# Key tiles of the shared keys and values made once, root rows instead of root columns in the sparse query stage, and identity products in the openings of a two-block transformer kernel

## The reference, cut to what matters

```python
def shared_kv(h, ...):                     # once, between the two layers
    u = modulate(rms_norm(h, kv_norm_g), shift, scale)
    kv = (u @ w_kv).reshape(b, s, 3, 2, N_KV_HEADS, HEAD_DIM)
    k_cmp = rms_norm(compress(kv[:, :, 0, 0], 0), kv_k_gain[0])   # silu(blocks @ phi_w1) @ phi_w2
    v_cmp = compress(kv[:, :, 0, 1], 1)
    k_slc = rope(rms_norm(kv[:, :, 1, 0], kv_k_gain[1]));  v_slc = kv[:, :, 1, 1]
    k_win = rope(rms_norm(kv[:, :, 2, 0], kv_k_gain[2]));  v_win = kv[:, :, 2, 1]
...
def nsa_mixer(u, ...):                     # the sparse attention
    qg = u @ w_qg
    q = rms_norm(qg[..., :hdim].reshape(b, s, N_HEADS, HEAD_DIM), q_gain)
    gates = jax.nn.sigmoid(qg[..., hdim:])
```

## Time and profile before

| what | value |
|---|---|
| median of 3 runs | 3850.7 us |
| profiled execution | 3850.64 us, of it span from the first to the last instruction 3848.9 us |
| mean granted TensorE clock | 0.971 of 2.4 GHz |
| PE busy | 3637.3 us (95%) |
| DVE busy, ACT busy | 1914.3 us (50%), 1422.3 us (37%) |
| DMA | 360.8 MB, 94 GB/s |

### The profile page before, as it was taken

The page is one execution under the profiler, slowest core; times in us unless marked ns, Lnnn a source line. Parts: engine busy times, 40 slices in busy tenths (PEclk is TensorE's granted clock), DMA queues, the critical chain, the costliest instruction groups (busy, mean ns, idle before and its releaser), DMA issues.

```text
span 3848.9 us, 49990 instructions
## 1 busy us (share of the span) xinstructions
PE 3637.3 (95%) x19328; PEld 2934.7 (76%) x19328; DVE 1914.3 (50%) x3874; ACT 1422.3 (37%) x2510; POOL 107.7 (3%) x183
## 2 busy tenths in 40 slices
PE   7879999989998999999999989999899998889999
PEld 6669956778887888777777768888788886668887
DVE  5757735555456545555545444333433345764332
ACT  3251212432233222555555543223322233863222
POOL 0000000010001000000000000000000000000000
PEclk9879999989998999999999999999899999999999
DMA  6200026234543544111111112222222221012222
GB/s 240 93 1 1 1 87 228 102 117 178 181 169 123 190 175 155 69 66 51 50 50 51 70 56 93 91 99 99 90 82 93 93 74 45 2 43 75 90 100 77
DMA packets 47159, 360.82 MB, mean 94 GB/s; under 512 B 5216, under 2 KB 5600, under 8 KB 28128
## 3 DMA queue, kind: packets, MB, share of 16 engines
q1 hardware_dynamic: 23472, 270.36, 19.1%
q0 software_dynamic: 23472, 87.50, 6.8%
HBM read 355.74 MB, written 2.10 MB: 93 GB/s over the span
## 4 chain that ended last, share of the span: by engine, by line
PE 84%; DVE 8%; issue 3%; ACT 3%; DVEq 1%; DMA 0%; PEld 0%; ACTq 0%; PEldq 0%; POOL 0%; SPq 0%; POOLq 0%
PE bank L798 21%; PE bank L803 21%; PE bank L804 21%; PE bank L1618 4%; PE bank L760 2%; PE bank L1951 1%; PE bank L1968 1%; PE bank L1939 1%; PE bank L2419 1%; PE bank L2386 1%; PE bank L1927 1%; DVE w_lo_sb L1220 1%; PE bank L778 1%; PE bank L2408 1%; PE bank L727 1%
## 5 line engine op out<-in xcount | busy, mean ns | idle before, releaser
L798 PE MATMUL bank<-x_hi_sb,w_hi_sb 128*128 128x512 f32 x2888 | 1155.2, 400 | 58.6 <-DVE w_lo_sb L1220 15.2
L804 PE MATMUL bank<-x_hi_sb,w_lo_sb 128*128 128x512 f32 x2888 | 1133.2, 392 | 0.0
L803 PE MATMUL bank<-x_lo_sb,w_hi_sb 128*128 128x512 f32 x2888 | 1132.8, 392 | 0.0
L798 PEld LDWEIGHTS bank<-x_hi_sb,w_hi_sb 128*128 128x128 f32 x2888 | 546.8, 189 | 208.8 <-issue 72.3
L1043 ACT ACTIVATE w_hi_sb<-slab_sb 128x1024 fp32r<-128x1024 f32 (+2 forms) x549 | 500.9, 936 | 502.7 <-PE bank L798 315.6
L1220 DVE TENSOR_TENSOR w_lo_sb<-slab_sb,w_hi_sb 128x1024 fp32r<-128x1024 f32 (+2 forms) x549 | 573.5, 1076 | 182.0 <-ACT w_hi_sb L1043 167.1
L804 PEld LDWEIGHTS bank<-x_hi_sb,w_lo_sb 128*128 128x128 f32 x2888 | 546.3, 189 | 117.4
L803 PEld LDWEIGHTS bank<-x_lo_sb,w_hi_sb 128*128 128x128 f32 x2888 | 547.5, 190 | 108.1
L1386 DVE TENSOR_TENSOR hid_sb<-silu_gate_sb,bank 128x512 f32<-128x512 f32 x110 | 75.6, 688 | 605.2 <-PE bank L804 605.2
L798 PE MATMUL bank<-hid_hi_sb,w_hi_sb 128*128 128x512 f32 x880 | 343.0, 390 | 0.0
L804 PE MATMUL bank<-hid_hi_sb,w_lo_sb 128*128 128x512 f32 x880 | 342.8, 390 | 0.0
(11 more groups left out here) (349 smaller groups left out, 3786.6 us busy)
## 6 DMA issues: line engine op xcount, KB each, us to landing
slab_sb<-weights SPq DMA_DIRECT2D x80, 2048.0 KB, 7.8
keep_sb<-ada POOLq DMA_DIRECT2D x133, 512.0 KB, 4.5
slab_sb<-weights SPq DMA_DIRECT2D x44, 1536.0 KB, 6.4
slab_sb<-weights SPq DMA_DIRECT2D x20, 1280.0 KB, 6.1
tables_sb<-ada POOLq DMA_DIRECT2D x14, 512.0 KB, 6.2
work_sb<-ada POOLq DMA_DIRECT2D x13, 512.0 KB, 7.6
h_sb<-x SPq DMA_DIRECT2D x4, 512.0 KB, 7.4
out<-h_sb SPq DMA_DIRECT2D x8, 256.0 KB, 2.7
```

The source lines that it names most:

```text
L798: mm = pe.matmul(out, w_hi[p][:, w], hi, start=first, stop=False)
L803: pe.matmul(out, w_hi[p][:, w], lo, start=False, stop=False)
L804: return pe.matmul(out, w_lo[p][:, w], hi, start=False, stop=last)
```

## The change

The weights of the two key projections are no longer written twice: one slab holds the selected key tile, the window key tile and the two compression tiles, and the values have a slab of their own (`w_v`). The second copies of the key heads are made by ACT at the end of the query stage. In the query stage the roots of a half are split into a high and a low part, turned into 16 rows (4 transposes), copied to SBUF by ACT, and each tile's bank is filled by one float32r product with a selector `pick`. The values take their banks one at a time. The two extra sums before the second opening are spread over the last products, one of them behind the stage's end. Identity products are added at twelve places. Cut to its core:

```diff
-    ("w_kv", 2, 4096),
+    ("w_kv", 1, 4096),
+    ("w_v", 1, 2048),
...
+        pick = sb("pick", [P, 4 * P], F32R)
+        root_parts = sb("root_parts", [P, NB, 16], F32R)
...
-        def pe_cols(e, sqv, tiles, nb, by_tile, sub):
+        def pe_cols(e, sqv, tiles, nb, by_tile, sub, busy):
...
             mm.then_inc(e.A.full[s], 1)
+            pe_stay_busy(e, busy)
             pe.wait_ge(inverted, e.nth(inverted))
...
+        def pe_turn_roots(e, ring, seat):
+            pe = e.eng
+            pe.wait_ge(parts_ready, e.nth(parts_ready))
+            s = e.give(ring, seat)
+            for b in range(NB):
+                mm = pe.transpose(ring.bank[s][0:16, b * P:(b + 1) * P], root_parts[:, b, :].bitcast(F32), ident)
+            mm.then_inc(ring.full[s], 1)
+        def pe_spread_rows(e, ring, seat, rows, j):
+            if j == 0:
+                e.eng.wait_ge(roots_turned, e.nth(roots_turned))
+            s = e.give(ring, seat)
+            n = S // len(rows)
+            for i, r in enumerate(rows):
+                mm = e.eng.matmul(ring.bank[s][:, i * n:(i + 1) * n], pick[0:16, j * P:(j + 1) * P], r, start=True, stop=True)
+            mm.then_inc(ring.full[s], 1)
+        def act_root_rows(e, ring, seat, rows):
...
+                x = act.activation(r, ring.bank[s][0:16, i * n:(i + 1) * n], ACT.Copy)
+            x.then_inc(roots_turned, 1)
+            act.drain().then_inc(ring.free[s], 1)
+        def dve_root_parts(e, src, tiles, sub):
...
+            e.link(dve.tensor_copy(hi, src), dve_step)
+            dve.tensor_tensor(lo, src, hi.bitcast(F32), ALU.subtract).then_inc(parts_ready, 1)
...
-            seats = [e.give(e.A, e.acc)] * NB if together else [e.give(e.A, e.acc) for _ in range(NB)]
+            seats = [e.give(e.A, e.acc)] * NB if together else []
             for i in range(parts):
                 p = e.take(part, e.part)
                 for b in range(NB):
+                    if len(seats) == b:
+                        seats.append(e.give(e.A, e.acc))
...
                     if sums and half == 1 and n == KT // 2 - 1:
+                        late = [lambda: pe_sums_open(e, cross, True),
+                                lambda: cross is not None and pe_sums_of(e, 1, cross[0])]
...
-            pe_cols(e, sq, 8, NB, False, 1)
+            pe_stay_busy(e, 16)
+            pe_cols(e, sq, 8, NB, False, 1, 18)
...
-            pe_cols(e, sq, 4, NB, False, 1)
+            pe_stay_busy(e, 10)
+            pe_cols(e, sq, 4, NB, False, 1, 6)
...
             e.stage_end("w_in")
+            pe_stay_busy(e, 40)
             e.stage_end("rope_tables")
             pe_swap(e, b1_qk, 6, wait=False)
+            pe_stay_busy(e, 20)
...
             e.stage_end("w_co")
+            pe_stay_busy(e, 4)
             pe_sums_close(e, crosses[0])
+            pe_stay_busy(e, 5)
             pe_rms_spread(e, rms=rms_add)
             pe_rms_spread(e)
+            pe_stay_busy(e, 20)
             pe_ffn(e, cross=crosses[1])
             e.stage_end("ffn_down")
-            pe_sums_close(e, crosses[1])
+            pe_stay_busy(e, 4)
+            pe_sums_close(e, crosses[1], (2,))
+            pe_stay_busy(e, 5)
             pe_rms_spread(e, rms=rms_add)
             pe_rms_spread(e)
+            pe_stay_busy(e, 20)
...
             pe_parts_opening(e, x_hi, x_lo)
             e.slab.next()
-            for _ in range(2):
-                pe_tile_parts(e)
-            pe_settle(e)
-            pe_head_cols(e, kv_sq, 4)
             pe_token_parts(e, 2, 2 * P, 2 * P)
             pe_settle(e)
-            pe.wait_ge(inverted, e.nth(inverted))
-            for j in range(4):
-                pe_spread(e, NB, 2, j)
+            pe_head_cols(e, kv_sq, 2)
...
             pe_slab(e, (), 0, 0, None, more=[compress])
-            pe_swap(e, kv_raw, 4)
+            pe.wait_ge(inverted, e.nth(inverted))
+            for j in range(2):
+                pe_spread(e, NB, 2, j)
+            pe_swap(e, kv_raw, 2)
...
             pe_head_cols(e, q_sq[:, 0:4, :], 4)
             pe_tile_parts(e)
             pe_settle(e)
-            pe.wait_ge(inverted, e.nth(inverted))
+            pe_turn_roots(e, e.A, e.acc)
+            pe_tile_parts(e)
             for j in range(4):
-                pe_spread(e, NB, 2, j)
-            pe_tile_parts(e)
+                pe_spread_rows(e, e.A, e.acc, rows_sparse, j)
...
-            pe.wait_ge(inverted, e.nth(inverted))
+            pe_turn_roots(e, e.A, e.acc)
             for j in range(4):
-                pe_spread(e, NB, 2, j)
+                pe_spread_rows(e, e.A, e.acc, rows_sparse, j)
```

More of the change, by code:

```diff
@@ L375, in two_blocks @@
         ident, ones1 = K("ident"), K("ones")[:, 0:1]
+        rows_dilated = [w_hi[i][0:16, QKV_PART:D] for i in (2, 3)]
+        rows_sparse = [root_rows[0:16, :]]
         acc = Ring(sem, "acc", 4)
@@ L819, in pe_parts @@
                         pe.wait_ge(ready, e.nth(ready))
-                    if late is not None and (t, kt) == (tiles - 1, nkt - 2):
-                        late()
+                    if late is not None and t == tiles - 1 and kt >= nkt - len(late):
+                        late[kt - nkt]()
                     mm = pe_product(e, s, p, slice(at * P, (at + 1) * P), hi[:, kt, :], lo[:, kt, :],
@@ L935, in pe_stay_busy, with pe_sums_of, pe_sums_open @@
                 e.eng.matmul(turn_bank[1][:, 0:P], ident, ident, start=True, stop=True)
-        def pe_sums_open(e, cross=None):
+        def pe_sums_of(e, n, tile):
+            for b in range(NB):
+                at = n * NB + b
+                e.eng.matmul(e.S.bank[e.sums][:, at:at + 1], tile[:, b * P:(b + 1) * P], ones1, start=at == 0, stop=False)
+        def pe_sums_open(e, cross=None, first=False):
             pe = e.eng
@@ L942, in pe_sums_open, with pe_sums_close @@
                 pe.wait_ge(summed, e.nth(summed))
-            for n, tile in enumerate([sq_sum] if cross is None else [sq_sum, cross[0], cross[1]]):
-                for b in range(NB):
-                    at = n * NB + b
-                    pe.matmul(e.S.bank[e.sums][:, at:at + 1], tile[:, b * P:(b + 1) * P], ones1, start=at == 0, stop=False)
-        def pe_sums_close(e, cross=None):
+            pe_sums_of(e, 0, sq_sum)
+            if cross is not None and not first:
+                pe_sums_of(e, 1, cross[0])
+                pe_sums_of(e, 2, cross[1])
+        def pe_sums_close(e, cross=None, left=()):
             pe = e.eng
+            for n in left:
+                pe_sums_of(e, n, cross[n - 1])
             for _ in range(KT):
@@ L1150, in act_ffn, with dve_invert @@
                 e.acc.pos += KT
-        def dve_invert(e, cols, factor=1.0, some=None):
+        def dve_invert(e, cols, factor=1.0, some=None, parts=None):
             dve = e.eng
@@ L1160, in dve_invert @@
                 r = dve.tensor_scalar(inv[:, 0:some], inv[:, 0:some], factor, None, ALU.mult)
-            r.then_inc(inverted, 1)
+            if parts is None:
+                r.then_inc(inverted, 1)
+            else:
+                e.link(r, dve_step)
+                parts(inv[:, 0:cols])
         def dve_add_normed(e, src, gain, after=None):
@@ L3095, in dve_run @@
             order = Order(e, KV_USES)
-            for q in range(PARTS):
-                dve_w_lo(e, q, D)
+            for q in range(2):
+                dve_w_lo(e, q, D, 1)
+            order.go("c1")
+            s = e.take(e.A, e.acc)
+            for kv in range(2):
+                for odd in range(2):
+                    dve.tensor_copy(kv_cmp[64 * odd:64 * odd + 64, 1, kv, 0:S - odd],
+                                    bank[s][64 * kv:64 * kv + 64, odd:S])
+            dve.drain().then_inc(e.A.free[s], 1)
             dve.wait_ge(hidden_ready, 1)
```

73 lines of the change are left out of this document (48 added, 25 removed).

## The result

The changed kernel takes 3824.63 us, the median of 4 runs (3823.66 to 3825.36), against 3850.41 us for the kernel before (4 runs, 3845.92 to 3850.93): a ratio of 0.9935 with a 95% interval of 0.9918 to 0.9953. The forecast was 3820 us with a range of 3808 to 3833. The profiled execution took 3824.53 us, 26.1 us under that of before, where the sum of the terms had said 30.3.

What follows compares the result with a forecast made beforehand. The prediction took PE, busy 95% of the span, and its time at the low granted clock to bound the kernel. Its terms summed to -30.3 us, from 3850.64 to 3820.3, rounded to 3820 us, range 3808 to 3833.

Steps and rivals of the forecast that it cites:

- (d): Rival, delta net: weight loads don't follow the clock, so gains of 3.8 and 3.0 us go; 3827 us, chance 0.04.
- (e): Rival, sparse queries: the row spreads' detour through DVE, PE and ACT eats what they save; 3822 us, chance 0.04.
- (a): Rival, keys' stage: gains only its two tiles, -10.9 us, as something else holds the next SwiGLU; 3828 us, chance 0.12.
- shared keys and values: Main term, keys' stage: two tiles, half the head sums, two spreads and low-clock time leave PE's path; -19.0 us.
- sparse queries: Query stage: first half's 64 spread passes become 4 transposes and 4 float32r products, second half +0.2 us; -1.7 us.
- delta net, first stage: Delta net preparation: identity products start the single-column burst high and let the spreads run high; -5.8 us.
- delta net, end: Delta net's end: 10 products make 32 passes run mostly high, six more overrun a short wait; -2.2 us.
- opening after w_co: First opening: added products on the path and overrunning a wait, against a faster opening behind; +0.5 us.
- opening after the first SwiGLU: Second opening: eight passes moved, added products' cost against spreads and opening partly at the high clock; -0.5 us.
- (c): Rival, identity products: they lift no clock and overrun short waits by 8.9 us; 3838 us, chance 0.08.
- (b): Rival, clock: the bursts hold the high level throughout, and so do the openings behind; 3799 us, chance 0.10.
- (f): Rival, slower: identity products run at the low level everywhere and overrun their waits, +28.7 us; 3858 us, chance 0.02.

Runs made afterwards that it cites:

- e1: The changed kernel without any of the identity products the change added; 3829.04 us, ratio 0.9946.
- e3: The changed kernel with the sparse queries' inverse roots spread by columns again, 64 passes a half; 3825.39 us, ratio 0.9936.
- e2: The changed kernel with the keys' 16 two-column head sums ahead of the values' 96 products instead of behind them; 3818.02 us, ratio 0.9917.
- e6: e2 with single identity products between every eight single-column products of the delta net's bursts, 3 in the first, 1 in the second; 3821.55 us, ratio 0.9929.
- e4: The kernel before with only the keys made once and the values' banks one by one; no row spreads, no added identity products; 3834.28 us, ratio 0.9957.
- e8: e2 with the second compression's weights in the values' slab, so the next SwiGLU's first weights load and split earlier; 3810.97 us, ratio 0.9902.
- e11: e9 without the 18 identity products behind the delta net's first burst, the 16 ahead kept; 3809.41 us, ratio 0.989.
- e7: e2 without the delta net's added identity products (16 and 18 in preparation, 10 and 6 at its end); 3824.37 us, ratio 0.9936.
- e5: e2 without the identity products added to the two openings (4, 5 and 20, twice); 3813.36 us, ratio 0.9905.
- e9: e8 without the identity products added to the two openings; 3808.82 us, ratio 0.9894.
- e12: e9 with two identity products between every four single-column products of the delta net's bursts, 14 in the first, 6 in the second; 3814.26 us, ratio 0.9907.
- e10: e9 without the rotary stage's 40 and 20 identity products; 3807.67 us, ratio 0.9896.

## Why the prediction was right, and where it was not

The total is inside the range, 4.6 us from the forecast. Three rivals are nearer by their number, (d) 3827, (e) 3822 and (a) 3828 us, but none describes what the traces show. That the sum came so near is in part luck: the terms that name an edit gained 22.9 of the 30.3 us, and stretches that no edit touches gave another 3.2. By its own steps, against the profiled execution:

| step | forecast | measured | by |
|---|---|---|---|
| shared keys and values | -19.0 | -13.2 | stretch; the same in e1 and e3 |
| sparse queries | -1.7 | -1.2 | stretch; -1.2 in e1, -1.1 in e2 |
| values' banks | -0.9 | -1.1 | stretch; in all 13 kernels |
| rotary stage | -0.9 | -1.4 | -0.9 to -1.5 in the others with it, 0.0 without |
| delta net, first stage | -5.8 | -4.6 | -6.2 to -6.5 in six others |
| delta net, end | -2.2 | -2.8 | to the middle of w_out; -0.6 to -2.8, -3.6 in e6 |
| opening after w_co | +0.5 | +0.6 | mean of six +1.1 |
| opening after the first SwiGLU | -0.5 | +1.0 | mean of six +0.3 |
| start | +0.2 | -0.3 | with the first stage |
| stretches that the change doesn't touch | 0 | -3.2 | see below |

**The step that failed** is the main term, -19.0 forecast and -13.2 measured. The parts that leave PE's path were costed rightly (18.0 forecast, 18.6 measured at the compression's start), and so was DVE's 1.2 us. The value products ran high, too. What failed is that the working ends there, with the 3.4 us at 0.50 gone, and puts what the moved burst does to the work behind it at nothing. The burst of head sums didn't vanish: now the compression stood directly behind it, and its price stayed at the 7.36 us of the earlier trace rows, which it had with 96 value products and 64 spreads ahead. It took 12.17 us, the spreads behind it 1.5 us more. Putting the sums back ahead of the values (e2) gave 19.9 us: the forecast's term was the price of an order that the change didn't write. e4 shows that it has nothing to do with the identity products.

**Rival (a)** gave a nearer size for this stretch (-10.9) for the wrong reason. More than the two tiles came through (half the head sums and all four early spreads did), and the compression and the spreads then gave 6.3 us back. Its mechanism, another hand-over that sets the end, is real all the same, and comes next: with the slab freed early the DMA is off the path, and ACT's and DVE's order holds the SwiGLU. e8 took that for another 4.9 us.

**The delta net** went by the mechanism named: the burst starts high and falls on the way, the spreads run high. Two sizes were off. The forecast let each microsecond at the high level save one; by its own prices (0.116 and 0.215 us) it saves 0.85, so its 3.8 us were worth 3.2, and the burst gained 2.7. And of the 3.0 us for the spreads half can come without the 18 products (8.82 us in e11) or without any (8.85 in e4), depending on when the level rises. The 18 products overran the reciprocal (done at 254.24, spreads from 255.48) by 1.2 us, close to the 1.0 forecast. Of the gain, 1.2 to 1.7 us are given back in the core behind, in every kernel but e1 and e7; e4, which came to it only 2.5 us earlier, gave back 1.3. Why is not shown.

**The openings** were forecast at 0 together. The measured cost of their products is 2.3 us, and leaving them out was right (e5, e9). In the timeline of the first opening the loss is the 4 products at the low level (1.92 us) and the 5 that overrun a short wait (2.48 against 0.57), more than the faster spreads (2.63 against 3.78) and the faster start of the SwiGLU give back.

**Rival (d),** weight loads that don't follow the clock, is refuted more sharply than by the rows of before. In e12 eight single-column passes took 0.95 us at 1.00 and 1.71 us at 0.50, in one burst: 0.119 against 0.214 us a pass.

```profile
242.60 0.95 PE L720 MATMUL bank<-const_sb,sq_sb 128*128 128x1 f32 x8
...
244.29 1.71 PE L720 MATMUL bank<-const_sb,sq_sb 128*128 128x1 f32 x8
```

The Trainium skill, TensorE: Matmul & The Clock Gate, section LDWEIGHTS (loading the stationary operand), gives columns over 1.2 GHz for a load, 107 ns for these 128 columns, with no clock level in it; the trace is near that at the high level and has twice that at the low one.

Of the others, (c) fell with e7, since the delta net's products give 6.35 us; (e) with the stretches of e3 and e4; (b) with the burst, which didn't stay high; (f) with the rotary stage's 80 passes, 9.17 us long and high throughout. In the queries' first half the working has a slip: 3.71 less 1.9 us is 1.8, not 1.9.

**What single microseconds are worth here.** The stretches that no edit touches moved, too. The clock of the kernel before and of the changed one over the same instructions of the dilated attention:

```profile
1802.00:1804.00 2.00, 1.44 (x4) 1.16 (x4) 0.48 (x1) 1.99 (x4) 0.00 (x0) 0.50 0.04 8
1804.00:1806.00 2.00, 2.00 (x6) 1.61 (x5) 0.48 (x1) 0.23 (x1) 0.00 (x0) 0.50 0.01 4
```

```profile
1795.00:1797.00 2.00, 1.68 (x7) 1.42 (x8) 0.59 (x1) 1.99 (x4) 0.00 (x0) 1.00 0.04 8
1797.00:1799.00 2.00, 2.00 (x10) 1.64 (x9) 0.37 (x1) 0.11 (x1) 0.00 (x0) 1.00 0.02 4
```

Around a wait of PE of 1.9 us (1.8 in the changed kernel) the level fell in one execution and not in the other, and the same work took 2.7 us less. Executions of one kernel differ by 2 us (e2) to 11 us (e6) and in one case 18 (e10), as much as an edit here is worth. Such places are the likely reason: e10's slowest execution had a mean granted clock of 0.972, its others 0.978 and 0.979; but only one execution of each kernel was traced. So e1's products are worth 9.2 us by one trace up to the keys and 4.4 by the medians, and so e3 and e10 were read by stretch. It also bears on the forecast itself: 3.2 of the 26.1 us came from stretches of no term, 3.3 gained in the dilated stage and the rest gains and losses that cancel.

What stays open: why the level falls 3.0 to 5.5 us into an unmixed burst and 7.8 us into a mixed one; when it rises under the spreads; and whether the gain in the dilated stage is chance or the effect of coming to it at another moment. Eight of the 13 kernels gained 2.6 to 3.8 us there and two some 1.1; e1 and e4, hardly earlier than the kernel before, gained nothing, but neither did e11, 9.8 us earlier. None of this was separated.

## What to carry to other kernels

When an edit shortens or moves work on TensorE, ask of each narrow burst what now stands directly ahead of it and behind it: two short-column bursts back to back fell to half clock, in four traces of four, while the same passes behind dense products did not, in nine of nine, and the mere order was worth 6.6 us. Identity products pay where a wait is longer than they are and a long run of passes follows (the delta net, 6.35 us) and cost where they stand on the path or overrun a short wait (the openings). With effects of 1 to 3 us and executions that differ by as much, compare the same instruction's start in several traces, stretch by stretch, before believing a median.

## What was not expected of the hardware

- A float32r product over 16 partitions with 512 columns takes about 0.24 us from start to start at the high level (three in 0.96 us with the last one's tail) and 0.43 us at the low one (four in 2.07 us).
- A burst of 64 single-column passes behind 3.8 us of identity products keeps the high level for 3.0 to 5.5 us (eight traces, 8.63 to 11.05 us long). With two identity products between every four single-column products it kept it for 7.8 us, and with one between every eight for no longer than without (4.4 us); but a burst of 32 passes with one in its middle ran high to its end, where it fell after 2.3 to 2.9 us without.
- Under spreads that start at the low level it rose after 3.0 us in e11 and 3.1 in e4 (8.82 and 8.85 us for 64 passes), and after 5.8 us in e7 and 6.2 in e1 (10.18 and 10.36). The burst ahead had been low from its start in e4, e7 and e1 alike.
- The level can fall around a wait of 1.9 us in one execution and stay in the next, with the same instructions: 2.7 us.
